# FFN gate and up of an encoder block by Strassen's scheme: seven block products in place of eight

## The reference, cut to what matters

```python
h2 = rmsnorm(x, norm2_g[l])
x = x + (jax.nn.silu(h2 @ w_ffn_gate[l]) * (h2 @ w_ffn_up[l])) @ w_ffn_down[l]
```

## Time and profile before

| | us |
|---|---|
| three runs: median (lowest to highest) | 710.99 (709.34 to 711.04) |
| the profiled execution: its own time | 708.88 |
| its span | 706.7 |

### The profile page before, as it was taken

One profiled execution on the slowest core, in us unless ns is written; L12 is line 12 of the kernel. 1 busy time (PEld: TensorE's weight loads), 2 busy tenths in 40 slices (PEclk: granted clock), 3 DMA queues, 4 the chain that ended last, 5 costly groups with the idle time before them and its releaser, 6 DMA issues.

```text
span 706.7 us, 9055 instructions
## 1 busy us (share of the span) xinstructions
PE 688.9 (97%) x3322; PEld 579.8 (82%) x3322; DVE 372.0 (53%) x607; ACT 333.1 (47%) x535; POOL 36.7 (5%) x42
## 2 busy tenths in 40 slices
PE   4999999999999999999999999999999999999996
PEld 4998888888888788888998888888888888888884
DVE  5676658787878895844633222222322243333346
ACT  6438577888877852324452333223332232232234
POOL 0000301111122200000000000000000000000000
PEclk9999999999999999999999999999999999999999
DMA  8242222111223145331332332322313323223103
GB/s 287 68 139 57 72 63 67 26 55 61 69 65 121 60 150 206 100 126 44 120 120 63 115 101 77 119 86 92 119 59 119 108 71 119 84 95 119 59 1 119
DMA packets 52886, 67.14 MB, mean 95 GB/s; under 512 B 5567, under 2 KB 43646, under 8 KB 52862
## 3 DMA queue, kind: packets, MB, share of 16 engines
q1 hardware_dynamic: 52846, 66.82, 29.2%
q10 hardware_dynamic: 16, 0.00, 0.0%
HBM read 64.72 MB, written 2.10 MB: 95 GB/s over the span
## 4 chain that ended last, share of the span: by engine, by line
PE 95%; ACT 2%; DVE 2%; DMA 1%; issue 0%; SPq 0%; ACTq 0%
PE ps L343 30%; PE ps L344 30%; PE ps L345 30%; PE ps L1321 2%; PE ps L1151 1%; PE ps L1271 1%; PE ps L1268 1%; DMA xt<-in_x_dram 1%; DVE hT_lo L804 1%; DVE w_lo L294 0%; ACT w_hi L284 0%; ACT prob L506 0%; PE ps L1233 0%; ACT hT_hi L520 0%; DVE f_lo L930 0%
## 5 line engine op out<-in xcount | busy, mean ns | idle before, releaser
L294 DVE TENSOR_TENSOR w_lo<-raw,w_hi 128x1024 fp32r<-128x1024 f32 (+2 forms) x117 | 140.1, 1201 | 200.4 <-ACT w_hi L284 199.2
L343 PE MATMUL ps<-hT_hi,w_lo 128*128 128x512 f32 (+1 forms) x608 | 224.6, 369 | 1.3 <-DVE hT_lo L804 0.6
L344 PE MATMUL ps<-hT_lo,w_hi 128*128 128x512 f32 (+1 forms) x608 | 223.1, 367 | 0.0
L345 PE MATMUL ps<-hT_hi,w_hi 128*128 128x512 f32 (+1 forms) x608 | 223.0, 367 | 0.0
L284 ACT ACTIVATE w_hi<-raw 128x1024 fp32r<-128x1024 f32 (+2 forms) x117 | 118.8, 1022 | 191.3 <-PE ps L345 185.2
L343 PEld LDWEIGHTS ps<-hT_hi,w_lo 128*128 128x128 f32 x608 | 114.6, 188 | 21.3 <-issue 2.1
L345 PEld LDWEIGHTS ps<-hT_hi,w_hi 128*128 128x128 f32 x608 | 114.6, 188 | 18.7
L344 PEld LDWEIGHTS ps<-hT_lo,w_hi 128*128 128x128 f32 x608 | 114.6, 189 | 18.5
L343 PE MATMUL ps<-w_hi,f_lo 128*128 128x512 f32 x180 | 70.0, 389 | 0.0
L344 PE MATMUL ps<-w_lo,f_hi 128*128 128x512 f32 x180 | 70.0, 389 | 0.0
L345 PE MATMUL ps<-w_hi,f_hi 128*128 128x512 f32 x180 | 70.0, 389 | 0.0
(11 more groups left out here) (154 smaller groups left out, 746.5 us busy)
## 6 DMA issues: line engine op xcount, KB each, us to landing
raw<-in_w_in_dram SPq DMA_DIRECT2D x12, 1024.0 KB
raw<-in_w_ffn_gate_dram SPq DMA_DIRECT2D x11, 1024.0 KB
raw<-in_w_ffn_up_dram SPq DMA_DIRECT2D x11, 1024.0 KB
raw<-in_w_ffn_down_dram SPq DMA_DIRECT2D x11, 1024.0 KB
raw<-in_w_out_dram SPq DMA_DIRECT2D x4, 1024.0 KB
xt<-in_x_dram SPq DMA_DIRECT2D x4, 512.0 KB, 6.0
raw<-in_w_o_lru_dram SPq DMA_DIRECT2D x2, 1024.0 KB
raw<-in_w_o_attn_dram SPq DMA_DIRECT2D x2, 1024.0 KB
```

The costliest lines, as they stand in the source:

```text
L294: last = nc.vector.tensor_tensor(split_view(w_lo, kind, t0 % 4), raw_view(kind, t0 // 2 % 2, t0 % 2), split_view(w_hi, kind, t0 % 4).bitca ...
L343: nc.tensor.matmul(dst, l_lo, r_hi, start=start, stop=False)
L344: nc.tensor.matmul(dst, l_hi, r_lo, start=False, stop=False)
L345: return nc.tensor.matmul(dst, l_hi, r_hi, start=False, stop=stop)
```

## The change

Features 0 and 1 stay as they were. The other 20 feature tiles are taken in ten steps; step n (j and par in the code, n = 2j + par) takes tiles 2 + n and 12 + n together. With W11, W12 the weights of the first of the two tiles for the inner halves 1 and 2, W21, W22 those of the second, and likewise four blocks of the activation (inner half, token half), the 2 x 2 block product is made by Winograd's form of Strassen's scheme: seven products of blocks in place of eight, for gate and for up, so 14 per step. A block product is 4 x 3 matmuls of 256 columns.

- **VectorE** makes three sums of weight blocks per matrix into `w_sum` (`sums`) and a fourth in place (`fourth`), once per step for gate and for up. It makes the four sums of the activation (t_one to t_four) once, ahead of and inside the first step. All sums are f32 and are split after the summing.
- **Tiles** of 1024 elements per step: a, b (raw W11 and W12 of gate and up), c, d, e (sums), f, g (a raw block and the fourth sum). Seven where there were four.
- **TensorE** accumulates `total`, `left` and `right` of gate (m = 0) and up (m = 1) in four banks, in the other four in the next step. Where a partial total is part of several results, it waits until ScalarE has copied it out (`keep`, counted by `st_copy`), and then goes on adding to it.
- **VectorE** adds copies and totals (`corner`, `row`), ScalarE takes silu, VectorE multiplies gate by up: three products per step.
- **Loads**: four transfers of 512 KB per step, into `raw` or (odd steps) into `scr`, which now holds several buffers of the earlier stages; a pair of steps ahead.
- **Order at the start**: the third tile's split stands ahead of the norm of token tile 3, ScalarE copies the first half's activation in f32 (`h32`) out of PSUM, and the second half's transposes stand behind the third tile.
- In **down**, names and counts of semaphores change (`down_hi`, `down_lo`), and its first two tiles are split within the last step. TensorE's matmuls are as before.

The diff, cut and moved to the left:

```diff
-T_DN = T_FFN + 2 * FT
+T_ST = T_FFN + 4
+STEPS, ST_TILES = (FT - 2) // 2, 7
+T_DN = T_ST + ST_TILES * STEPS
...
+h32 = store[:, 18:22, :].rearrange("p a (b n) -> p (a b) n", b=2)
+t_one = store[:, 8:10, :].rearrange("p a (b n) -> p (a b) n", b=2)
+t_two = store[:, 10:12, :].rearrange("p a (b n) -> p (a b) n", b=2)
+t_three, t_four = h32[:, 0:4, :], h32[:, 4:8, :]
+w_sum = scr[:, 8:14, :]
+part_one = [scr[:, 14, :], scr[:, 15, :]]
+part_two = [scr[:, 16, 0:256], scr[:, 16, 256:512]]
+gate_21 = scr[:, 17, 0:256]
...
+ST_SLOT = {"a": 0, "b": 1, "c": 2, "d": 3, "e": 0, "f": 1, "g": 2}
...
+def st_raw(par, m):
+    flat = raw[:, m, :] if not par else scr[:, 4 * m:4 * m + 4, :].rearrange("p a n -> p (a n)")
+    return flat.rearrange("p (k i n) -> p k i n", k=KD, i=2)
+def st_source(par, tile):
+    if tile in "ab":
+        return st_raw(par, "ab".index(tile))[:, :, 0, :]
+    if tile in "cd":
+        c = 2 * "cd".index(tile)
+        return w_sum[:, c:c + 2, :]
+    if tile == "e":
+        return w_sum[:, 4:6, :]
+    return st_raw(par, "fg".index(tile))[:, 4:8, :, :]
...
+    def load_blocks(par, m, j):
+        for i, first in enumerate((2, 2 + STEPS)):
+            sync.dma_start(st_raw(par, m)[:, :, i, :],
+                           (w_fu_v if m else w_fg_v)[:, :, bass.ds(j * 256 + P * (first + par), P)]).then_inc(
+                               st_in[par][m], 16)
+    for m in range(2):
+        sync.wait_ge(w_ready, T_FFN + 2 * m + 2)
+        load_blocks(0, m, 0)
+    for m in range(2):
+        load_blocks(1, m, 0)
+    with sync.Fori(1, STEPS // 2) as j:
+        for par in range(2):
+            for m in range(2):
+                sync.wait_ge(w_ready, st_count("fg"[m], j, par - 2))
+                load_blocks(par, m, j)
...
+    split_hi(act, T_FFN + 2)
     norm_square(3)
     root(2, 3, 1, 7)
-    for t in (2, 3):
-        split_hi(act, T_FFN + t)
+    for d in range(KD):
+        nc.scalar.activation(h32[:, d, :], ps[:, d // 2, 256 * (d % 2):256 * (d % 2) + 256], ACT.Copy,
+                             scale=prm[:, ROW_G2 + d:ROW_G2 + d + 1]).then_inc(h32_ready, 1)
+    split_hi(act, T_FFN + 3)
     norm_hi(ROW_G2, 0, 1, KD, h2_half)
...
-    def ffn(i, i0):
-        for j in range(2):
-            tile_used(act, i * 4 + T_FFN + j)
...
+    def block_hi(tile, j, par, first=False):
+        if first:
+            tile_used(act, T_FFN + ST_SLOT[tile])
+        else:
+            previous, back = ST_PREVIOUS[tile]
+            st_used(act, previous, j, par - back)
+        if tile in "ab":
+            act.wait_ge(st_in[par]["ab".index(tile)], j * 32 + 32)
+        else:
+            act.wait_ge(st_sum, j * 16 + 8 * par + {"c": 3, "d": 6, "e": 5, "f": 7, "g": 8}[tile])
+        nc.scalar.activation(st_split(w_hi, tile), st_source(par, tile), ACT.Copy).then_inc(w_half, 1)
+    def first_silu(n):
+        tile_used(act, T_FFN + n)
+        nc.scalar.activation(silu[:, n, :], ps[:, 4 + n, :], ACT.Silu).then_inc(silu_ready, 1)
+    def t_hi(q, src, count):
+        act.wait_ge(t_full, count)
+        nc.scalar.activation(t_block(f_hi, q), src, ACT.Copy).then_inc(t_half, 1)
+    def keep(dst, bank, col):
+        nc.scalar.activation(dst, ps[:, bank, col:col + 256], ACT.Copy).then_inc(st_copy, 1)
+    def step(j, par, first=False, last=False):
+        b, nj, npar = 4 * par, (j + 1 if par else j), 1 - par
+        block_hi("c", j, par, first)
+        block_hi("d", j, par, first)
+        if first:
+            t_hi(2, t_three, 9)
+        block_hi("e", j, par)
+        act.wait_ge(act_ready, j * 6 + 3 * par + 2)
+        keep(part_one[0][:, 0:256], b, 0)
+        block_hi("f", j, par)
+        if first:
+            t_hi(3, t_four, 10)
+        keep(part_one[1][:, 0:256], b + 2, 0)
+        block_hi("g", j, par)
+        keep(part_one[0][:, 256:512], b, 0)
+        keep(part_two[0], b + 1, 256)
+        st_used(act, "d", j, par)
+        keep(part_one[1][:, 256:512], b + 2, 0)
+        keep(part_two[1], b + 3, 256)
+        if last:
+            act_hi(0)
+            act_hi(1)
+        act.wait_ge(st_22, j * 4 + 2 * par + 1)
+        nc.scalar.activation(part_two[0], part_two[0], ACT.Silu).then_inc(st_silu, 1)
+        if last:
+            down_hi(0)
+        else:
+            block_hi("a", nj, npar)
+        st_used(act, "f", j, par)
+        nc.scalar.activation(gate_21, ps[:, b, 0:256], ACT.Silu).then_inc(st_silu, 1)
+        if last:
+            down_hi(1)
+        else:
+            block_hi("b", nj, npar)
+        act.wait_ge(st_row, j * 4 + 2 * par + 1)
+        nc.scalar.activation(part_one[0], part_one[0], ACT.Silu).then_inc(st_silu, 1)
+    block_hi("a", 0, 0, first=True)
+    first_silu(0)
+    t_hi(0, t_one, 4)
+    t_hi(1, t_two, 8)
+    block_hi("b", 0, 0, first=True)
+    first_silu(1)
+    step(0, 0, first=True)
+    step(0, 1)
+    with act.Fori(1, STEPS // 2 - 1) as j:
+        for par in range(2):
+            step(j, par)
+    step(STEPS // 2 - 1, 0)
+    step(STEPS // 2 - 1, 1, last=True)
...
+    split_lo(dve, T_FFN + 2)
     norm_begin(2, 3, 4 * NT)
     norm_end(2, 3, xn[:, 3, :], 7)
-    for t in (2, 3):
-        split_lo(dve, T_FFN + t)
+    split_lo(dve, T_FFN + 3)
     norm_lo(ROW_G2, 0, 1, h2_half, h2_ready)
...
+    def half_one(d, f32, dst, done):
+        src = ps[:, d // 2, 256 * (d % 2):256 * (d % 2) + 256]
+        nc.vector.scalar_tensor_tensor(dst, src, prm[:, ROW_G2 + d:ROW_G2 + d + 1], f32, ALU.mult,
+                                       ALU.subtract).then_inc(done, 1)
+    def t_lo(q, src):
+        dve.wait_ge(t_half, q + 1)
+        nc.vector.tensor_tensor(t_block(f_lo, q), src, t_block(f_hi, q).bitcast(F32),
+                                ALU.subtract).then_inc(t_split, 1)
+    def sums(m, j, par):
+        v, c = st_raw(par, m), 2 * m
+        w11, w21, w22 = v[:, 0:4, 0, :], v[:, 0:4, 1, :], v[:, 4:8, 1, :]
+        def out(slot):
+            return w_sum[:, slot, :].rearrange("p (k n) -> p k n", k=4)
+        dve.wait_ge(st_in[par][m], j * 32 + 32)
+        nc.vector.tensor_tensor(out(c), w21, w22, ALU.add).then_inc(st_sum, 1)
+        nc.vector.tensor_tensor(out(4 + m), w11, w21, ALU.subtract).then_inc(st_sum, 1)
+        dve.wait_ge(st_sum, j * 16 + 8 * par + 3 * m + 1)
+        nc.vector.tensor_tensor(out(c + 1), out(c), w11, ALU.subtract).then_inc(st_sum, 1)
+    def fourth(m, j, par):
+        w12 = st_raw(par, m)[:, 4:8, 0, :]
+        dve.wait_ge(st_sum, j * 16 + 8 * par + 3 * m + 3)
+        dve.wait_ge(w_ready, st_count("ab"[m], j, par))
+        nc.vector.tensor_tensor(w12, w12, w_sum[:, 2 * m + 1, :].rearrange("p (k n) -> p k n", k=4),
+                                ALU.subtract).then_inc(st_sum, 1)
+    def first_product(n):
+        dve.wait_ge(silu_ready, n + 1)
+        tile_used(dve, T_FFN + 2 + n)
+        nc.vector.tensor_tensor(store[:, n, :], silu[:, n, :], ps[:, 6 + n, :], ALU.mult).then_inc(act_ready, 1)
+    def corner(m, j, par):
+        if m:
+            st_used(dve, "e", j, par)
+        else:
+            dve.wait_ge(st_third, j * 2 + par + 1)
+        dve.wait_ge(st_copy, j * 12 + 6 * par + 4 + 2 * m)
+        nc.vector.tensor_tensor(part_two[m], part_two[m], ps[:, 4 * par + 2 * m, 0:256], ALU.add).then_inc(st_22, 1)
+    def row(m, j, par):
+        st_used(dve, "fg"[m], j, par)
+        nc.vector.tensor_tensor(part_one[m], part_one[m], ps[:, 4 * par + 2 * m + 1, :], ALU.add).then_inc(st_row, 1)
+    def step(j, par, first=False, last=False):
+        nj, npar = (j + 1 if par else j), 1 - par
+        feature = j * 2 + par + 2
+        block_lo("c", j, par)
+        block_lo("d", j, par)
+        if first:
+            first_product(1)
+            dve.wait_ge(t_full, 8)
+            nc.vector.tensor_tensor(t_three, t_two, h32[:, 0:4, :], ALU.subtract).then_inc(t_full, 1)
+            t_lo(2, t_three)
+        block_lo("e", j, par)
+        if first:
+            for m in range(2):
+                fourth(m, 0, 0)
+            nc.vector.tensor_tensor(t_four, h32[:, 4:8, :], t_two, ALU.subtract).then_inc(t_full, 1)
+        elif not last:
+            dve.wait_ge(w_ready, st_count("e", j, par))
+            sums(0, nj, npar)
+        block_lo("f", j, par)
+        if first:
+            t_lo(3, t_four)
+            dve.wait_ge(w_ready, st_count("e", j, par))
+            sums(0, nj, npar)
+        elif not last:
+            sums(1, nj, npar)
+        block_lo("g", j, par)
+        corner(0, j, par)
+        if first:
+            sums(1, nj, npar)
+        corner(1, j, par)
+        if last:
+            act_lo(0)
+            act_lo(1)
+            down_lo(0)
+        else:
+            block_lo("a", nj, npar)
+        dve.wait_ge(st_22, j * 4 + 2 * par + 2)
+        dve.wait_ge(st_silu, j * 6 + 3 * par + 1)
+        nc.vector.tensor_tensor(store[:, feature + STEPS, 256:512], part_two[0], part_two[1],
+                                ALU.mult).then_inc(act_ready, 1)
+        row(0, j, par)
+        if last:
+            down_lo(1)
```

(100 more changed lines are left out.)

141 lines of the change are left out of this document (83 added, 58 removed).

## The result

The changed kernel takes 698.71 us (median of 4 runs, 698.27 to 698.77), the kernel before beside it 710.29 (709.34 to 711.04): 0.984 of its time, 95% interval 0.983 to 0.986. The profiled execution took 698.77, with a span of 696.7; the forecast was 700.0, and 698.7 for the profiled one.

A forecast was written before the change was run, and what follows sets the result against it. TensorE, busy 97% of the span, was taken as the bound. -16.0 + 5.8 = -10.2 us took the profiled 708.88 to 698.7, or 700.8 from the median; forecast 700.0, 8-in-10 range 694 to 708.

The forecast's parts named there:

- TensorE's part, -16.0: Gate and up loop: 168 matmuls at 0.120 us, 20.16 us per step against 21.76, saving 16.0 us over ten steps.
- Steady step at no cost: Steady steps of the loop: TensorE's 20.16 us hides VectorE's 16.0 and ScalarE's 10.1, so they cost nothing.
- the walk: Steady step's queues followed in order: last product ends at 2.4 us, corner 0 at 13.2, smallest margin 0.7 at copy 5.
- The table load every second step: ScalarE in the loop: a 1.28 us load at the first silu of a block of straight code, every second step.
- Entry, loads, way down at no cost: Before the first step, the weight transfers and the down stage: each costs nothing, first step reached at 362.65 us.
- First step, +5.8: First of the ten steps: ScalarE's late copies idle TensorE 3.7 and 2.0 us, so it takes 20.2 + 5.8 us.
- the first stall: First step: copy 1 ready at 373.4, wanted by TensorE at 369.8, 3.7 us idle.
- The second stall: First step: copy 2, behind f and the fourth block, ready at 378.3, wanted at 376.4, 2.0 us more idle.
- The rival of the clock: Clock falls in the first step's idle, costing 1.5 us and up to 3, whole 701.5 to 703; chance 0.14.
- The rival of VectorE as the bound: From corner 1 to next step's c split: VectorE sets the step, deciding from 21.2 us, whole 715 to 722; chance 0.10.
- 1.3 times the sum of the rows: VectorE's work per step, summed at 16.0 us from recorded rows, at which it would decide, 21.2 us per step.
- this margin (2.0): Steady step: tightest of VectorE's leads over TensorE on tiles c to g, 2.0 us.

The follow-up runs named there:

- halves256: Kernel before, each of the twenty gate and up loop tiles computed as two halves of 256 tokens: 723.24 us against 709.72, ratio 1.019.
- the rerun: The changed kernel run once more, unaltered, on the chip of a later follow-up run: 699.78 us, ratio to the kernel before 0.986.
- filled: Changed kernel with sixteen unread 512-column matmuls keeping TensorE busy during the first step's wait for copy 1: 700.35 us.
- reordered2: reordered, plus first two activation blocks' high parts ahead of blocks a and b on ScalarE, both plain tiles' silu behind them: 698.68 us.
- six_before_c: Changed kernel with six unread 128 x 512 VectorE operations ahead of c's low part in the nine later steps: 711.64 us, ratio to before 1.003.
- reordered: Changed kernel, first step only: ScalarE's bank copies ahead of splits not yet needed, VectorE's second plain product earlier, next step's sums later: 698.65 us, ratio to before 0.984.
- level: reordered2 with VectorE's and ScalarE's first-step order changed again, both fourths earlier and corner 0 ahead of next step's sums: 693.57 us, ratio to before 0.977.
- dve4: Changed kernel with four unread 128 x 512 VectorE operations ahead of c's low part in every step: 702.91 us, ratio to before 0.992.

## Why the prediction was right, and where not

- **TensorE's part, -16.0.** Right. 168 matmuls take 20.16 us in each of nine steps. halves256 shows by itself the price of the narrow shape from which it came. The formula of the Trainium skill, "TensorE: Matmul & The Clock Gate" (Back-to-back issue gap), by which the step would save 2.4 us, is out: the traces say 1.60, and the measurement decides. The same section of the Trainium skill calls it the gap of an isolated matmul, and says that against a stream with weight loads it counts too little at small widths and too much at large ones; here it counts 11 ns too little at both.
- **Steady step at no cost.** Right, and so was the walk: last product 2.2 us into the next step (2.4), corner 0 at 13.3 (13.2), c ahead by 2.5 (2.0), copy 5 done at 421.03 for 421.91, 0.9 ahead (0.7). The table load every second step was wrong: the trace has one, ahead of the first silu. Nothing hung on it.
- **Entry, loads, way down at no cost.** Right: the first step starts at 362.50 (362.65), the 512 KB transfers land in 4.7 to 6.1 us against a lead of 17, and the way down takes the same 119.5. The 2 us of the later starts arise in the first 18 us of the execution.
- **First step, +5.8.** Right in size, 6.13 (5.74 in the rerun), and in the first stall: copy 1 wanted at 369.7, TensorE on again at 373.35 (369.8 and 373.4). The second stall was not there as forecast. Copy 2 ended at 378.17 (378.3), but TensorE, at the lower clock, came for it only at 378.64; filled brings the stall back at 1.9 us (2.0).
- **The rival of the clock** happened, in the place named, and still cost next to nothing. Its price of 1.5 to 3 us was right for the matmuls alone (2.5), but I added it to a sum that held the second stall already: the lower clock and that stall fill the same time. By filled the net is 0.4 us, and nothing against the rerun. Where nothing is due behind it, it costs in full (1.5 us in reordered2). The section "HAM oscillation" of the same page of the Trainium skill says that idle gaps return the engine to the lower level. These idles of 3.65 us agree with it; an idle of 1.3 us in each of nine steps (six_before_c) did not do it.
- **What the prediction did not see** is behind the stalls. It read the first step as two late copies. reordered took both away and gained 0.5 us (0.1 against the rerun): VectorE, on which the activation's sums and splits lie in that step, was as late at corner 0. Only when its order too followed TensorE's wants did the 5.4 us go (level, against the rerun).
- **The rival of VectorE as the bound** was rightly unlikely, and it named the right place, the stretch ahead of c's split. Its step length of 21.2 us, at which the gain is gone, fits too: six_before_c, at 21.55, is no faster than before. What was wrong is the work that it takes to get there, "1.3 times the sum of the rows". VectorE delays TensorE as soon as the last product and c's split exceed c's 5.76 us, which is with 2.2 to 2.4 us more work per step ahead of c. dve4, with 2.4, costs 0.18 us in each of the eight later steps; six_before_c, with 3.6, loses the gain. The walk had this margin (2.0); the rival should have been priced by it instead of by the sum.
